# Finer waits at four seams of a two-block kernel, and filter generation moved ahead of the inverse transform's matmul

## The chip, the cores and the metric

The kernel runs on one core of a Trainium2 chip, as one launch. The metric is the device time of an execution in microseconds (us). Three runs of the kernel before took 3126.72, 3129.09 and 3131.32 us; their median is 3129.09 us.

The engines in the text: PE (TensorE matmul, with PEld its weight loads), DVE (VectorE), ACT (ScalarE), POOL (GpSimd) and SP (SyncE). POOL and SP issue the DMAs. Each engine runs its own instructions in the order in which they are written, and waits on counting semaphores.

## The reference

Input x is 2048 rows by 1024 channels, float32. A first block (banded attention and a pooled path) is followed by a second, in which the whole change lies. Cut to what matters:

```python
h = rms_norm(x, pre_norm_w)
proj = h @ w_in                       # 1024 -> 7168
hy_in, hy_gate, sg_u, sg_v, sg_gate = split(proj)
hy_in = short_conv_centred(hy_in, conv_w, conv_b)   # u[t-1]*w0 + u[t]*w1 + u[t+1]*w2 + b
x0, x1, v = split(hy_in, 3)
k = hyena_filter(...)                 # 3-layer sine MLP -> (4096, 1024) samples, * decay, / l1 norm
y_a = x0 * long_conv_bidir(v * x1, k, hyena_skip) * silu(hy_gate)   # FFT convolution over 4096
# spatial gating: per head (8 heads of 128), LayerNorm of sg_v, then a 128 x 128 mix along time
mixed = einsum('hpq,bnqhd->bnphd', sgu_w, vc) + sgu_b
y_b = sg_u * mixed * silu(sg_gate)
x = x + rms_norm(concat(y_a, y_b) @ w_out, post_norm_w)
```

## The kernel before

The second block has three parts, which follow one another in program order; between blocks of the program all engines meet.

**Projections (some 970 to 2242 us).** After the values (sg_v) the projections run as a list of tiles, each 128 output channels by 2048 rows in four PSUM banks, two tiles in flight (banks 0 to 3 and 4 to 7). A projection tile takes 8 x 4 x 3 matmuls (lines L1845 to L1847, high and low halves of the operands). The first 24 tiles are, for each head h, `gate`, `mix`, `u`; the rest are, for each channel group e, `x0`, `hgate`, `x1`, `v` (with one tile `third` of the filter network). Before PE writes tile j it waits for the evacuation of tile j-2 (`banks_free`).

- A `mix` tile is 16 matmuls (L1822) over VN, the normalised values of one head. POOL loads VN in one DMA of 1024 KB (L1666), double buffered; VN lies over the output buffer of the head before, so that the load for head h first waits until the result of head h-1 is stored. PE waits for the whole load.
- A convolution tile (`x0`, `x1`, `v`) is evacuated by ACT with the middle tap (L1715), then DVE adds the two outer taps (L1740, L1743). For `v` DVE then forms the product (L1784) that SP stores.
- DVE puts 6 to 14 operations of the filter network's first layer (`filter_work`, L120 to L143) behind each tile, and splits the weights of the tile after next (L1730).

**Long convolution (2242 to 2770 us), `long_convolution`.** Channels go in four chunks of 256 (NCH = 4). The 32 filter samples of a chunk are generated in 16 steps: PE `generate` (L2332) into one PSUM bank, DVE `weighted` times the decay (L2176), ACT absolute value (L2086), DVE `summed` (L2185). For the first chunk this is done up front. For the later ones one step lies in each of the 16 pairs of the chunk before. `generate(n + 16)` waits until `weighted(n + 15)` has read the bank.

Pair n of a chunk is: PE `forms` (L2406: filter spectrum, then input spectrum), ACT four copies of the filter spectrum (L2124, L2126), DVE three products and a difference (L2263, L2264, L2265, L2267), then `weighted` and `summed`; PE `inverse` (L2390), ACT `inverse_out` (L2106). PE runs ahead by one: in step p it issues forms(p+1), inverse(p-1), generate(p+16). ACT's order is the copies of pair p, inverse_out(p-1), absolute value, copies of pair p+1.

Between two chunks PE transforms the next filter (`filter_first`, L2344, 16 groups, four banks ahead of DVE's transposes L2193 in `filter_turned`), transposes the next inputs (`inputs_turn`, L2367), runs `inverse_first` (L2432) and `inputs_first` (L2377). DVE also turns the outputs (`outputs_turned`, L2210), the inputs (`inputs_turned`, L2202), and applies `gate` (L2227) and `gate_product` (L2239).

**Output projection (2742 to 3128 us)**, L2532 to L2534, which the change doesn't touch.

Of the kernel before, what the change touches and what calls it, by code (L numbers as in the profile page):

```python
# [9 lines left out]
ALU = mybir.AluOpType  # L10
# [5 lines left out]
S = 2048  # L16
# [1155 lines left out]
def second_inputs(nc, A, PS, first, first_ctx, CC, HP, kept, h1_d, h2_d, vn_d, bi_d, u_d, gx_d, yb_d, wv_d):  # L1172

    with ExitStack() as outer:
# [404 lines left out]
        with ExitStack() as ctx:  # L1579
# [10 lines left out]
            sgt_in = [stage_sem("sgt_in%d" % i) for i in range(2)]  # L1590
            vn_in = stage_sem("vn_in")
            mix_gated = stage_sem("mix_gated")
# [9 lines left out]
            arg3_done = stage_sem("arg3_done")  # L1602
            sin3_done = stage_sem("sin3_done")
            CONV = ("x0", "x1", "v")
            CONV_AT = {"x0": 0, "x1": 1, "v": 0}
# [45 lines left out]
            @block.gpsimd  # L1651
            def _(g):
                values_gpsimd(g)
                for b in range(2):
                    g.wait_ge(vn_stored[b], 16 * NT)
                g.wait_ge(sv_done, STEPS)
                g.sem_clear(first.semaphores)
                vnr = vn_d.rearrange("(i p) (h d) -> h p i d", p=P, d=P)
                for h in range(8):
                    if h >= 2:  # L1660
                        g.wait_ge(sgu_done, h - 1)
                    g.dma_start(SGT[:, h % 2], A["sgu_w_2"][h]).then_inc(sgt_in[h % 2], 16)
                    g.dma_start(BI[:, h % 2], bi_d[h]).then_inc(sgt_in[h % 2], 16)
                    if h:
                        g.wait_ge(yb_stored[(h + 1) % 2], 16 * ((h + 1) // 2))
                    g.dma_start(VN[h % 2], vnr[h]).then_inc(vn_in, 16)  # L1666

            @block.scalar
            def _(s):
# [10 lines left out]
                for j, (kind, n, _) in enumerate(tiles):  # L1680
# [7 lines left out]
                    if kind not in ("u", "mix"):  # L1688
                        s.wait_ge(tile_done, j + 1)
# [7 lines left out]
                    elif kind == "hgate":  # L1697
                        if n:
                            s.wait_ge(u_stored, 16 * n)
                        else:  # L1700
                            s.wait_ge(yb_stored[1], 64)
                        s.activation(AB[1], ps, ACT.Silu).then_inc(evac_done, 1)
                    elif kind in CONV:
                        which = CONV.index(kind)
# [17 lines left out]
            def _(v):  # L1722
# [10 lines left out]
                def outer_taps(which, n, j):  # L1733
# [11 lines left out]
                    v.wait_ge(taps_done, conv + 1)  # L1745

                def second_angle():
# [18 lines left out]
                for j, (kind, n, _) in enumerate(tiles):  # L1766
# [5 lines left out]
                    elif kind == "mix":  # L1772
# [6 lines left out]
                        v.wait_ge(evac_done, evacs_before(j))  # L1779
                        v.tensor_tensor(AB[n % 2], ps, AB[n % 2], ALU.mult).then_inc(mix_gated, 1)  # L1780
                    elif kind in CONV:
                        outer_taps(CONV.index(kind), n, j)
# [17 lines left out]
            def _(t):  # L1800
# [13 lines left out]
                for j, (kind, n, _) in enumerate(tiles):  # L1814
# [3 lines left out]
                    if kind == "mix":  # L1818
                        t.wait_ge(sgt_in[n % 2], 32 * (n // 2 + 1))
                        t.wait_ge(vn_in, 16 * (n + 1))  # L1820
                        for i in range(NT):
                            ins = t.matmul(PS[:, banks + i // 4, P * (i % 4):P * (i % 4) + P], VN[n % 2][:, i], SGT[:, n % 2],  # L1822
                                           start=True, stop=True)
# [7 lines left out]
                    else:  # L1831
                        w = slot_of[j]
                        t.wait_ge(wl_done, NV + w + 1)
                        for c in range(NTC):
# [7 lines left out]
                            for k in range(KD):  # L1842
# [4 lines left out]
                                ins = t.matmul(dst, wl, hh, start=False, stop=(k == KD - 1))  # L1847
                    ins.then_inc(tile_done, 1)

# [22 lines left out]
def long_convolution(nc, A, CC, HP, KX, M, PS, kept, L, gx_d, u_d, ya_d, yb_d):  # L1872

    with ExitStack() as ctx:
# [287 lines left out]
        def _(v):  # L2162
# [41 lines left out]

            def outputs_turned(ug):
                cc, ct = ug // 2, ug % 2
                v.wait_ge(z_done, 16 * cc + 16)
                for h in range(2):
                    c = P * ct + 64 * h
                    v.transpose(KTC[cc % 2][:, c:c + 64], UTC[:, c:c + 64]).then_inc(it_done, 1)  # L2210
# [44 lines left out]
            for cc in range(NCH):  # L2255
# [33 lines left out]
                if cc + 1 < NCH:  # L2289
# [3 lines left out]
                    summed(16 * cc + 31)  # L2293
                    filter_turned(cc + 1, range(2, 8))
                outputs_turned(2 * cc)
                if cc + 1 < NCH:
                    filter_turned(cc + 1, range(8, 16))
                    norm(cc + 1)
# [11 lines left out]
        def _(t):  # L2310
# [45 lines left out]
            def inputs_turn(ug):  # L2356
                t.wait_ge(uin_in, 16 * (ug + 1))
                if ug % 2 == 0:
                    t.wait_ge(kt_done, 8 * ug + 16)
                else:  # L2360
                    t.wait_ge(ut_done, 4 * ug)
                for q in range(4):
# [31 lines left out]
            def second_stage(cc):  # L2394
# [469 lines left out]
```

## Time and profile before

| | us |
|---|---|
| median of three runs | 3129.09 |
| the profiled execution, its own time | 3130.32 |
| its span | 3128.5 |
| PE busy | 2982.3 (95%) |
| DVE busy | 2531.5 (81%) |
| ACT busy | 827.0 (26%) |
| granted PE clock, mean share of full speed | 0.987 |

The span is the time between the first and the last recorded instruction; 1.8 us of the execution lie around it. A PE idle time is given with the engine, DMA or tile that ended it.
### The profile page before, as it was taken

The numbers are of one execution on the slowest core, as the hardware profiler recorded it, in microseconds if no ns is written. First come the engines' busy times: TensorE is split into PE (matmuls) and PEld (weight loads), VectorE is DVE, ScalarE is ACT, GpSimd is POOL, SyncE is SP. The second block draws the span as 40 slices with busy tenths as digits, with TensorE's granted clock in tenths as the row PEclk, the third lists the DMA queues.
The fourth block names the chain that finished last, engine by engine and source line by source line (L and its number), as shares of the span: only waits on it lengthen the run. The fifth ranks groups of instructions, "written<-read, shape, count | busy, mean of one in ns | idle before, by whom it ended". The sixth has DMA issues, their size and how long they took to land. (4 is left out here: it accounts for less than half of the span.)

```text
span 3128.5 us, 33046 instructions
## 1 busy us (share of the span) xinstructions
PE 2982.3 (95%) x12866; PEld 2163.7 (69%) x12866; DVE 2531.5 (81%) x2789; ACT 827.0 (26%) x1402; POOL 336.1 (11%) x458
## 2 busy tenths in 40 slices
PE   8999999999998999999999999999899989889999
PEld 4444444656777887888888888887656656678887
DVE  7979999898996869999999999998477979762221
ACT  3000000696334320000011111112343735631111
POOL 2211121001333430000000000000000100000000
PEclk9999999999999999999999999999999999989999
DMA  7675553201457546565554454541222331454331
GB/s 214 180 172 158 174 151 79 115 1 65 148 186 241 145 134 171 150 182 141 153 140 139 122 152 135 141 141 34 109 86 81 110 120 42 148 168 124 92 108 41
DMA packets 212115, 406.39 MB, mean 130 GB/s; under 512 B 21008, under 2 KB 134328, under 8 KB 204088
## 3 DMA queue, kind: packets, MB, share of 16 engines
q1 hardware_dynamic: 189256, 324.58, 34.2%
q0 software_dynamic: 21552, 71.32, 8.4%
q10 hardware_dynamic: 1152, 8.39, 0.7%
q8 instruction: 102, 1.67, 0.2%
q14 instruction: 53, 0.43, 0.0%
HBM read 324.53 MB, written 85.98 MB: 131 GB/s over the span
## 5 line engine op out<-in xcount | busy, mean ns | idle before, releaser
L1845 PE MATMUL PS<-HX,WH 128*128 128x512 f32 x1536 | 599.4, 390 | 6.9 <-DVE MB L1743 5.0
L1847 PE MATMUL PS<-HX,WL 128*128 128x512 f32 x1536 | 598.3, 390 | 0.0
L1846 PE MATMUL PS<-HX,WH 128*128 128x512 f32 x1536 | 598.3, 390 | 0.0
L849 PE MATMUL PS<-M 128*128 128x512 f32 x1088 | 472.0, 596 | 7.5 <-DVE M L650 6.3
L849 PEld LDWEIGHTS PS<-M 128*128 128x128 f32 x1088 | 207.4, 191 | 271.9 <-issue 263.7
L1845 PEld LDWEIGHTS PS<-HX,WH 128*128 128x128 f32 x1536 | 288.9, 188 | 67.9 <-DVE MB L1743 5.9
L1846 PEld LDWEIGHTS PS<-HX,WH 128*128 128x128 f32 x1536 | 288.9, 188 | 59.9
L1847 PEld LDWEIGHTS PS<-HX,WL 128*128 128x128 f32 x1536 | 288.7, 188 | 60.0
L120 DVE SCALAR_TENSOR_TENSOR HP<-MF,HP 128x1024 f32<-128x1024 f32 x252 | 323.5, 1284 | 8.0
L120 DVE SCALAR_TENSOR_TENSOR M<-M 128x1024 f32<-128x1024 f32 x160 | 205.6, 1285 | 26.5 <-DMA M<-c_feat 20.9
L2532 PE MATMUL PS<-WH,YH 128*128 128x512 f32 x512 | 202.1, 395 | 8.9 <-DVE HP L2671 5.2
L2533 PE MATMUL PS<-WH,YL 128*128 128x512 f32 x512 | 201.4, 393 | 0.0
L2534 PE MATMUL PS<-WL,YH 128*128 128x512 f32 x512 | 201.2, 393 | 0.0
L2655 DVE TENSOR_TENSOR YL<-KX,YH 128x2048 fp32r<-128x2048 f32 x14 | 32.1, 2292 | 205.2 <-ACT YH L2634 205.2
L1715 ACT ACTIVATE MB<-PS,MF 128x2048 f32<-128x2048 f32 x24 | 49.6, 2066 | 444.5 <-PE PS L1847 444.5
L2062 POOL DMA_DIRECT2D M<-c_decay x48 | 25.8, 538 | 1095.7 <-DVE KX L2176 893.9
L72 POOL DMA_DIRECT2D M<-c_feat x186 | 94.9, 515 | 382.5 <-DVE M L120 361.8
L2532 PEld LDWEIGHTS PS<-WH,YH 128*128 128x128 f32 x512 | 97.4, 190 | 31.6 <-issue 7.4
L1530 PE MATMUL PS<-WVH,HX 128*128 128x512 f32 x256 | 101.4, 396 | 14.2 <-DVE HX L1454 6.0
L1028 DVE TENSOR_TENSOR M<-M 128x1024 f32<-128x1024 f32 x90 | 110.1, 1223 | 2.4
L2534 PEld LDWEIGHTS PS<-WL,YH 128*128 128x128 f32 x512 | 97.4, 190 | 20.4
L2533 PEld LDWEIGHTS PS<-WH,YL 128*128 128x128 f32 x512 | 97.4, 190 | 20.3
(224 smaller groups left out, 5060.7 us busy)
## 6 DMA issues: line engine op xcount, KB each, us to landing
MF<-h_scratch SPq DMA_DIRECT2D x380, 256.0 KB, 4.3
M<-c_feat POOLq DMA_DIRECT2D x186, 256.0 KB, 4.4
MF<-w_in SPq DMA_DIRECT2D x52, 512.0 KB, 4.8
M<-u_scratch SPq DMA_DIRECT2D x16, 1024.0 KB, 4.9
M<-c_decay POOLq DMA_DIRECT2D x48, 256.0 KB, 2.9
M<-x SPq DMA_DIRECT2D x18, 512.0 KB, 4.1
M<-w_in SPq DMA_DIRECT2D x18, 512.0 KB, 5.9
x_scratch<-M SPq DMA_DIRECT2D x16, 512.0 KB, 5.0
```

The costliest lines, as they stand in the source:

```text
L72: eng.dma_start(dst[HID * half:HID * half + HID], row).then_inc(loaded, 16)
L120: return v.scalar_tensor_tensor(out=out, in0=a, scalar=s_, in1=b, op0=op0, op1=op1)
L849: ins = t.matmul(ps[:, c, :], wt[:, k], HT[:, k, TC * c:TC * c + TC], start=(k == 0), stop=(k == KD - 1))
L1028: link(v.tensor_tensor(out, a, b, op))
L1530: t.matmul(dst, hh, wh, start=(k == 0), stop=False)
L1715: s.activation(AB[CONV_AT[kind]], ps, ACT.Identity, bias=w[:, 3:4], scale=w[:, 1:2]).then_inc(evac_done, 1)
L1845: t.matmul(dst, wh, hh, start=(k == 0), stop=False)
L1846: t.matmul(dst, wh, hl, start=False, stop=False)
L1847: ins = t.matmul(dst, wl, hh, start=False, stop=(k == KD - 1))
L2532: t.matmul(dst, yh, wh, start=(n == 0), stop=False)
L2533: t.matmul(dst, yl, wh, start=False, stop=False)
L2534: return t.matmul(dst, yh, wl, start=False, stop=(n == KY - 1))
```

## The change

Five edits, all in the second block:

1. VN is loaded by two DMAs of 8 time blocks each, with a semaphore each; PE waits for the second ahead of the ninth matmul of a `mix`.
2. The last projection tile (`v`, 7) is evacuated in two halves of 1024 columns: ACT, two taps and product for the first half once PE has finished its two banks, then for the second.
3. In `outputs_turned` for the chunk's first 128 channels the two transposes are put apart: after filter groups 0 to 5 and 0 to 10, where both stood behind group 7.
4. `inputs_turn` for the odd channel group waits for three of the four transposes of the even one; `inputs_first` waits for the fourth ahead of its second group.
5. In the pairs of the first three chunks `generate` stands in front of `inverse`.

```diff
@@ gpsimd, loads of the mix
-                    g.dma_start(VN[h % 2], vnr[h]).then_inc(vn_in, 16)
+                    for half in range(2):
+                        g.dma_start(VN[h % 2][:, 8 * half:8 * half + 8], vnr[h][:, 8 * half:8 * half + 8]).then_inc(vn_in[half], 16)
@@ scalar
+                    elif (kind, n) == LAST_TILE:
...
+                        for half in range(2):
+                            s.wait_ge(last_half_done, half + 1)
+                            part = slice(1024 * half, 1024 * half + 1024)
+                            s.activation(AB[0][:, part], ps[:, part], ACT.Identity, bias=w[:, 3:4], scale=w[:, 1:2]).then_inc(last_evac, 1)
@@ vector
+                def last_tile(ps, w):
+                    dst = AB[0]
+                    for half, (lo, hi) in enumerate(((0, 1023), (1023, S))):
+                        first, end = 1024 * half, 1024 * half + 1024
+                        v.wait_ge(last_evac, half + 1)
+                        v.scalar_tensor_tensor(out=dst[:, max(first, 1):end], in0=ps[:, max(first, 1) - 1:end - 1], scalar=w[:, 0:1],
+                                               in1=dst[:, max(first, 1):end], op0=ALU.mult, op1=ALU.add).then_inc(last_tap, 1)
...
+                        ins = v.tensor_tensor(AB[1][:, lo:hi], dst[:, lo:hi], AB[1][:, lo:hi], ALU.mult)
+                    ins.then_inc(u_done, 1)
@@ tensor, a mix tile
-                        t.wait_ge(vn_in, 16 * (n + 1))
                         for i in range(NT):
+                            if i % 8 == 0:
+                                t.wait_ge(vn_in[i // 8], 16 * (n + 1))
@@ vector, between two chunks
-                    filter_turned(cc + 1, range(2, 8))
-                outputs_turned(2 * cc)
-                if cc + 1 < NCH:
-                    filter_turned(cc + 1, range(8, 16))
+                    filter_turned(cc + 1, range(2, 6))
+                    outputs_turned(2 * cc, (0,))
+                    filter_turned(cc + 1, range(6, 11))
+                    outputs_turned(2 * cc, (1,))
+                    filter_turned(cc + 1, range(11, 16))
                     norm(cc + 1)
@@ inputs_turn
-                    t.wait_ge(ut_done, 4 * ug)
+                    t.wait_ge(ut_done, 4 * ug - 1)
@@ inputs_first
+                    elif g == 1 and ug % 2:
+                        t.wait_ge(ut_done, 4 * ug)
@@ second_stage, the loop over pairs
+                    if cc + 1 < NCH:
+                        generate(n + 16)
                     if p >= lag_of(cc):
                         inverse(n - lag_of(cc))
-                    if cc + 1 < NCH:
-                        generate(n + 16)
```

On PE, in a pair of the first chunk, the rows before are these (L2406 is forms, L2390 inverse, L2332 generate):

```order
L2390 MATMUL PS<-M3 128x256 x2
L2332 MATMUL PS<-M3,HP 64x256 x4
L2406 MATMUL PS<-KX,M3 128x256 x2
L2406 MATMUL PS<-M3 128x256 x2
L2390 MATMUL PS<-M3 128x256 x2
```

And these in the changed kernel, where L2442 is forms, L2366 generate and L2426 inverse:

```order
L2442 MATMUL PS<-KX,M3 128x256 x2
L2442 MATMUL PS<-M3 128x256 x2
L2366 MATMUL PS<-M3,HP 64x256 x4
L2426 MATMUL PS<-M3 128x256 x2
L2442 MATMUL PS<-KX,M3 128x256 x2
```

The four matmuls of generate now stand between forms and the inverse of the pair before.

On DVE, between the first and the second chunk, the rows before are these (L2193 turns filter groups, L2185 adds up absolute values, L2210 turns outputs, L2215 and L2217 are the norm):

```order
L2193 STREAM_TRANSPOSE M<-PS 128x16x16x2
L2185 TENSOR_TENSOR M<-M 128x512
L2193 STREAM_TRANSPOSE M<-PS 128x16x16x2 x6
L2210 STREAM_TRANSPOSE KX<-M 128x64x16x2 x2
L2193 STREAM_TRANSPOSE M<-PS 128x16x16x2 x8
L2215 TENSOR_SCALAR M<-PS 128x1 x2
L2217 RECIPROCAL M<-M 128x2
```

And these in the changed kernel (L2226 filter groups, L2243 outputs, L2248 and L2250 the norm):

```order
L2226 STREAM_TRANSPOSE M<-PS 128x16x16x2
L2218 TENSOR_TENSOR M<-M 128x512
L2226 STREAM_TRANSPOSE M<-PS 128x16x16x2 x4
L2243 STREAM_TRANSPOSE KX<-M 128x64x16x2
L2226 STREAM_TRANSPOSE M<-PS 128x16x16x2 x5
L2243 STREAM_TRANSPOSE KX<-M 128x64x16x2
L2226 STREAM_TRANSPOSE M<-PS 128x16x16x2 x5
L2248 TENSOR_SCALAR M<-PS 128x1 x2
```

The two long transposes, which stood together behind filter group 7, now have five filter groups between them.

## Rows read from the trace of the kernel before

**Rows 1.** Who waited for whom, PE: us in total, times, longest us.

```profile
PE PS L1822 <- DMA MB<-vn_scratch: 10.7, 4, 3.1
PE PS L2332 <- PEq L1579: 10.1, 1, 10.1
PE PS L2367 <- DVE M L2202: 5.7, 4, 1.4
```

**Rows 2.** PE in a pair, timeline: start us, us, engine, line, operation.

```profile
2326.41 1.13 PE L2332 MATMUL PS<-M,HP 64*64 64x256 f32 x8
2327.47 1.18 PE L2406 MATMUL PS<-KX,M 128*128 128x256 f32 x4
...
2329.40 1.07 PE L2390 MATMUL PS<-M 128*128 128x256 f32 x4
2330.39 1.13 PE L2332 MATMUL PS<-M,HP 64*64 64x256 f32 x8
```

**Rows 3.** DVE in the same pair, timeline.

```profile
2328.23 0.69 DVE L2267 TENSOR_TENSOR M<-M 128x512 f32<-128x512 f32 x1
2328.84 0.68 DVE L2176 TENSOR_TENSOR M<-PS,M 128x512 f32<-128x512 f32 x1
...
2330.08 0.69 DVE L2263 TENSOR_TENSOR M<-PS,M 128x512 f32<-128x512 f32 x1
```

**Rows 4.** ACT in the same pair, timeline; in brackets idle before, and releaser.

```profile
2327.56 1.19 ACT L2124 ACTIVATE M<-PS 64x512 f32<-64x512 f32 x2
2328.78 1.21 ACT L2126 ACTIVATE M<-PS 64x512 f32<-64x512 f32 x2
2330.50 0.65 ACT L2106 ACTIVATE M<-PS 128x512 f32<-128x512 f32 x1 [0.51 <-PE PS L2390]
```

**Rows 5.** PE windows, first chunk's generation: stretch, length, busy, clock, DMA share, GB/s.

```profile
2250.00:2266.00 16.00, 12.12 (x88) 1.00 0.76 308
```

**Rows 6.** PE and DVE timeline between two chunks; DVE's waits, 2377 to 2393.

```profile
2386.62 5.41 PE L2344 MATMUL PS<-M 128*128 128x512 f32 x8 [2.33 <-DVE M L2193]
2381.50 4.46 DVE L2210 STREAM_TRANSPOSE KX<-M 128x2048 f32<-128x2048 f32 x2
DVE M L2193 <- PE PS L2344: 1.7, 3, 1.0
```

**Rows 7.** Windows of PE at two places behind a wait.

```profile
2388.00:2390.00 2.00, 2.00 (x4) 0.50 0.00 0
...
1303.00:1305.00 2.00, 2.00 (x11) 0.50 1.03 240
```

**Rows 8.** Input transposes between two chunks, PE and DVE, timeline.

```profile
2411.57 1.14 PE L2367 MATMUL PS<-M 128*128 128x128 f32 x8 [1.44 <-DVE M L2202]
2408.43 1.25 DVE L2202 STREAM_TRANSPOSE M<-PS 128x1024 f32<-128x1024 f32 x1 [0.49 <-PE PS L2377]
```

**Rows 9.** Last projection tile: ACT and DVE, timeline; a 1024-wide operation by form.

```profile
2232.64 2.06 ACT L1715 ACTIVATE MB<-PS,MF 128x2048 f32<-128x2048 f32 x1 [19.69 <-PE PS L1847]
2239.57 2.29 DVE L1784 TENSOR_TENSOR MB<-MB 128x2048 f32<-128x2048 f32 x1
L2671 DVE SCALAR_TENSOR_TENSOR HP<-PS,SSQ,KX 128x1024 f32<-128x1024 f32 x16 | 20.5, 1284 | 44.8 <-POOL SSQ L2627 44.8
```

**Rows 10.** ACT behind the tiles of heads 2 and 3, timeline; POOL's load.

```profile
1252.63 1.88 ACT L1694 ACTIVATE MB<-PS 128x2048 f32<-128x2048 f32 x1 [20.70 <-PE PS L1847]
...
1277.97 1.06 ACT L1672 ACTIVATE WH<-MF 128x1024 fp32r<-128x1024 f32 x1 [22.52 <-PE PS L1847]
1299.73 1.88 ACT L1694 ACTIVATE MB<-PS 128x2048 f32<-128x2048 f32 x1 [20.70 <-PE PS L1847]
...
1329.15 1.06 ACT L1672 ACTIVATE WH<-MF 128x1024 fp32r<-128x1024 f32 x1 [26.60 <-PE PS L1847]
1291.70 1.17 POOL L1666 DMA_DIRECT2D MB<-vn_scratch  x1 [47.34 <-DMA yb_scratch<-MB]
```

**Rows 11.** DVE's waits from 1204 to 1504 us.

```profile
DVE WL L1730 <- ACT WH L1672: 7.9, 3, 3.0
```

More of the change, by code:

```diff
@@ L1590, in second_inputs @@
             sgt_in = [stage_sem("sgt_in%d" % i) for i in range(2)]
-            vn_in = stage_sem("vn_in")
+            vn_in = [stage_sem("vn_in%d" % i) for i in range(2)]
             mix_gated = stage_sem("mix_gated")
@@ L1603, in second_inputs @@
             sin3_done = stage_sem("sin3_done")
+            last_half_done = stage_sem("last_half_done")
+            last_evac = stage_sem("last_evac")
+            last_tap = stage_sem("last_tap")
+            LAST_TILE = ("v", 7)
             CONV = ("x0", "x1", "v")
@@ L1687, in _ @@
                         s.activation(L3[2][HID:P, 1:S], L3[1][HID:P, S - 1:0:-1], ACT.Sin).then_inc(sin3_done, 1)
-                    if kind not in ("u", "mix"):
+                    if kind not in ("u", "mix") and (kind, n) != LAST_TILE:
                         s.wait_ge(tile_done, j + 1)
@@ L1702, in _ @@
                         s.activation(AB[1], ps, ACT.Silu).then_inc(evac_done, 1)
+                    elif (kind, n) == LAST_TILE:
+                        w = CW[:, 8 * CONV.index(kind) + n]
+                        s.wait_ge(gx_stored, 16 * (n + 1))
+                        for half in range(2):
+                            s.wait_ge(last_half_done, half + 1)
+                            part = slice(1024 * half, 1024 * half + 1024)
+                            s.activation(AB[0][:, part], ps[:, part], ACT.Identity, bias=w[:, 3:4], scale=w[:, 1:2]).then_inc(last_evac, 1)
                     elif kind in CONV:
@@ L1745, in outer_taps @@
                     v.wait_ge(taps_done, conv + 1)
+                def last_tile(ps, w):
[5 more added lines that the diff above has]
+                                               in1=dst[:, max(first, 1):end], op0=ALU.mult, op1=ALU.add).then_inc(last_tap, 1)
+                        v.wait_ge(last_tap, 2 * half + 1)
+                        stop = min(hi, S - 1)
+                        v.scalar_tensor_tensor(out=dst[:, lo:stop], in0=ps[:, lo + 1:stop + 1], scalar=w[:, 2:3],
+                                               in1=dst[:, lo:stop], op0=ALU.mult, op1=ALU.add).then_inc(last_tap, 1)
+                        v.wait_ge(last_tap, 2 * half + 2)
+                        ins = v.tensor_tensor(AB[1][:, lo:hi], dst[:, lo:hi], AB[1][:, lo:hi], ALU.mult)
+                    ins.then_inc(u_done, 1)
                 def second_angle():
@@ L1780, in _ @@
                         v.tensor_tensor(AB[n % 2], ps, AB[n % 2], ALU.mult).then_inc(mix_gated, 1)
+                    elif (kind, n) == LAST_TILE:
+                        last_tile(ps, CW[:, 8 * CONV.index(kind) + n])
                     elif kind in CONV:
@@ L1847, in _ @@
                                 ins = t.matmul(dst, wl, hh, start=False, stop=(k == KD - 1))
-                    ins.then_inc(tile_done, 1)
+                            if (kind, n) == LAST_TILE and c % 2:
+                                ins.then_inc(last_half_done, 1)
+                    if (kind, n) != LAST_TILE:
+                        ins.then_inc(tile_done, 1)
             first_ctx.close()
@@ L2203, in inputs_turned, with outputs_turned @@
                                 PS[:, 2 * (g % 2):2 * (g % 2) + 2, :].rearrange("p x (c i) -> p c x i", i=16)).then_inc(ut_done, 1)
-            def outputs_turned(ug):
+            def outputs_turned(ug, halves=(0, 1)):
                 cc, ct = ug // 2, ug % 2
                 v.wait_ge(z_done, 16 * cc + 16)
-                for h in range(2):
+                for h in halves:
                     c = P * ct + 64 * h
```

## The prediction

> **What bounds the kernel now.** I read the engines' busy shares first: PE has work in 95% of the span, so only what PE waits for, or how slowly it is clocked, can be won. Then the list of PE's waits [rows 1]: 10.7 us for the loads of the mix tiles, one wait of 10.1 us at the seam between projections and convolution, 5.7 us in four waits for turned inputs. Then the timeline of each of these places, and last, since edit 5 moves work in 45 pairs, the timeline of one pair on three engines [rows 2 to 4]. There the reader is to see that a pair takes 3.98 us: generate starts at 2326.41 and again at 2330.39 [rows 2], and no idle time stands before PE's or DVE's rows [rows 2, 3]. ACT waits 0.51 us for inverse in each pair [rows 4].
>
> **Edit 5, generate ahead of inverse.** Generate takes 1.06 us (2326.41 to the next start, 2327.47), inverse 0.99 (2329.40 to 2330.39) [rows 2]. PE's own sum doesn't change. What changes is a circle of waits over two pairs. Follow it: inverse starts; ACT's inverse_out starts 1.10 later (2329.40 to 2330.50) [rows 2, 4]; inverse_out and the absolute value take 1.04 (the period of 3.98 less the four copies, 2327.56 to 2328.78 + 1.21 = 2.43, less the idle 0.51) [rows 4]; the four copies 2.43; DVE's products start 0.09 behind them (2329.99 to 2330.08) [rows 3, 4]; DVE ends weighted 3.42 after it began its pair (2330.08 less 3.98 is 2326.10; 2328.84 + 0.68 is 2329.52) [rows 3]. So from inverse(p-1), in PE's step p, to weighted of pair p+1 there are 1.10 + 1.04 + 2.43 + 0.09 + 3.42 = 8.08 us. PE's step p+2 then issues generate, which must wait for that weighted (one bank), some 0.06 more, and inverse(p+1).
>
> Before, inverse comes first and needs only the difference, which DVE finishes 0.60 ahead of weighted (2328.23 + 0.69 is 2328.92) [rows 3]; the circle is then 8.08 - 0.60 + 0.06 = 7.54 for two pairs, under the 7.96 that PE's own work takes, so it doesn't bind. After, generate stands in the circle: 8.08 + 0.06 + 1.06 = 9.20 for two pairs, 4.60 per pair, over 3.98. Neither ACT nor DVE can shorten it, because each executes in order: the copies of pair p+1 are queued behind inverse_out(p-1) on ACT, and DVE's next pair behind the copies. The circle starts with the chunk's first generate that waits. The pairs 0 and 1 start as before; pair 2 starts when its copies, queued behind inverse_out(0), are done: weighted(0) at DVE's start + 3.42, 0.06 + 1.06 for generate, then 1.10 + 1.04 + 2.43 + 0.09, together 9.20 behind the start of pair 0; by the same sum it was 7.54. From pair 3 to pair 15 lie six more circles. That makes 1.66 at the start and 6 x (9.20 - 7.96) = 7.44: 9.1 us per chunk, for three chunks +27.3. A generate that has waited may be slower by 0.1, as its weights aren't loaded ahead: 0.7 per chunk. From below the bound is 0 (the circle doesn't close), from above 31. I take +27.5. Nothing hides it: the transform of the next filter waits for the last weighted of the chunk, and the last chunk, without generate, isn't touched.
>
> **Edit 3, halves of the turned outputs.** PE waits 2.33 us for a turned filter group behind DVE's two long transposes (4.46), and its eight instructions then take 5.41 us [rows 6]; for four of these microseconds it is at 1.2 GHz in part, [rows 7] show 0.50. PE could win 2.33 and some 1.9 of clock, 4.2 in all. But DVE has all 16 groups and the same 4.46 to do, and what follows waits for its last group. It is idle 1.7 us in this stretch [rows 6], and by my estimate some 0.6 more between the first eight groups, where it follows PE in steps under the list's threshold. So DVE bounds the gain at 2.3. In the new order it comes to that: half a transpose (2.2) lies under three matmul groups of PE. -2.3 three times, -7; bounds -5 and -12.
>
> **Edit 4.** PE waits 1.44 us for the fourth input transpose [rows 8], in all 5.7 at four places [rows 1]. The third has ended at 2408.43 + 1.25 = 2409.68, before PE's preceding matmuls are issued (about 2410.0), so the wait goes wholly, with some 0.1 of restart: -1.5 four times, -6. The fourth is late next only for inputs_first, 25 us on. Bounds: 0 and -6.4.
>
> **Edit 2, the last tile.** From PE's end the path is ACT 2.06 (from 2232.64), two taps, the product (to 2239.57 + 2.29 = 2241.86): 9.2 us [rows 9]. The first half now runs under PE's second (half of a tile's 21 us, the idle time of ACT before such a tile's end in [rows 10]). The second half costs: ACT 1.05, taps 1.28 each by the 1024-wide form, product 1.22 (half of 2.29 and a little) and 0.2 of releases: 5.0 [rows 9]. -4.2. DVE is idle there, so nothing is queued behind. Bounds -3.5 and -4.6. The clock falls in the remaining wait as before.
>
> **Edit 1, halves of the mix loads.** Behind an even head gate and u end 25.34 us apart (1252.63 to 1277.97), behind an odd one 29.42 (1299.73 to 1329.15) [rows 10]. Of the 4.08 the wait for the load is some 2.2 by the timeline (on average 10.7 / 4 = 2.7 [rows 1]); the rest is clock: 0.50 from 1303 on [rows 7]. If each of the four odd heads loses that, it is 16.3 in all, of which 10.7 are waits [rows 1]. The load takes 10.2 us (from 1291.70 to the end of PE's wait, 1299.7 + 2.2) [rows 10]; its first half should be there some 4 us earlier, an estimate from half of that, and eight matmuls of 0.23 then cover 1.9 of what is left. But DVE has little room: it waited 7.9 us in three waits, one per two heads [rows 11], so that two heads can shrink by 2.6 at most, and the load itself starts behind DVE's product. So: 2.6 three times at the most for heads up to 6, and 3 to 4 for head 7, behind which the convolution tiles leave DVE room: 11. If the clock still falls behind the second half's wait, 1.9 each is kept, partly under DVE: 7. I take -9.5, between; bounds 0 and -14. SP and its queue aren't touched; POOL issues two DMAs for one, and nothing is queued behind them that is due.
>
> **The sum.** +27.5 - 7 - 6 - 4.2 - 9.5 = +0.8 us on the profiled execution's 3130.3: 3131.1. That execution lies 1.2 over the median of the runs shown, so 3129.9 in terms of the median. A measurement of this kernel can tell about 0.2%, 6.3 us, from no change.
>
> **Rivals.** (a) The pairs keep their 3.98 us: the circle is not closed, since a wait that I read as binding is met early. Then edit 5 costs nothing, perhaps wins the 1.4 us waits at the chunks' ends, and the time is 3129.9 - 27.5 = 3102. For it speaks that ACT has 0.51 us idle per pair and PE waits for inverse at the ends of the chunks; against it that DVE starts 0.09 behind ACT's copies already, without room.
>
> (b) Slower: DVE paces the gate, mix and u tiles. The place is heads 0 to 7, the price is that edit 1 gives back at most 1 instead of 9.5: 3129.9 + 9 = 3139. For it: a DVE waiting only 7.9 us in 300 [rows 11], and a second half that lands no earlier than the whole did. Against: the clock cost, which is PE's own. It is slower than before beyond the 6.3 from the point where edit 1 gives less than 4.
>
> (c) The clock falls in the pairs. They would have idle of about 1.2 us in 9.2. In the first chunk's generation PE is busy 12.12 of 16 us in short pieces and keeps 1.00 [rows 5]; one fall costs about 1.9, as at the mixes, and a fall per circle, 21 times, would add 40 and give 3170. The Trainium skill speaks for this one: its page "TensorE: Matmul & The Clock Gate", section "A second HAM failure mode: psum-queue depth-cycling", says that short idles between groups of matmuls, from cycling through PSUM banks, can make the clock oscillate. The trace agrees that waits can bring the clock down [rows 7], but not in a stretch that is busier on average than the one of [rows 5].
>
> **Numbers.** Forecast 0.67, with an own range of 3121 to 3139; (a) 0.14; (b) 0.14; (c) 0.05. Within the forecast the sizes of edits 1 and 5 are each uncertain by 4 or so, together 6: of its 0.67 some 0.49 lies within 6.3 us, 0.10 under and 0.08 over. Rival (a) adds 0.14 to faster, (b) 0.05 to same and 0.09 to slower, (c) 0.05 to slower. Faster 0.24, same 0.54, slower 0.22. The range 3115 to 3141 leaves out most of (a) and (c).
>
> **What would show it.** In the changed profile: DVE's first product of every second pair 9.2 us apart instead of 7.96; PE idle before generate, released by weighted, of about 1.2 every second pair, and none before inverse at the chunks' ends but the last. No wait of 2.3 us in the filter's transform, and the clock at 1.00 there. Four waits for input transposes gone. The seam's wait 5.9 us instead of 10.1. At the odd mixes no wait before the first matmul, one of some 1 to 2.5 before the ninth. Pairs at 3.98 us would make the forecast wrong by the whole of edit 5, and odd heads that still take 29 us by edit 1.

## The result, and the profile after

The changed kernel takes 3147.64 us (median of 4 runs, 3144.01 to 3151.18) against 3128.42 of the kernel before on the same chip: ratio 1.0056, 95% interval 1.0043 to 1.0068. It is 19.2 us slower, 17.7 over the forecast of 3129.9 and outside the range, and it is slower where no change was forecast. The profiled execution took 3146.14 us.

The engines' busy times on the page of the changed kernel, and its clock in the view of the cores:

```profile
PE 2995.2 (95%) x12866; PEld 2171.8 (69%) x12866; DVE 2531.6 (81%) x2792; ACT 826.2 (26%) x1403; POOL 341.1 (11%) x466
...
core 0: 3144.3 us, clock 0.984
```

DVE has the same work as before. PE has 12.9 us more (2982.3 before), though the change adds no matmul to it, and its clock went from 0.987 to 0.984. Busy time that grows without work is the first sign of a lower clock.

PE's waits in the changed kernel (us in total, times, longest us), where L2366 is generate, L1852 the mix and L2442 forms:

```profile
PE PS L2366 <- DVE M L2209: 22.6, 16, 3.1
PE PS L2366 <- DVE KX L2209: 14.5, 19, 2.7
PE PS L2366 <- PEq L1579: 6.0, 1, 6.0
PE PS L2442 <- DVE M L2235: 5.7, 4, 1.4
...
PE PS L1852 <- DMA MB<-vn_scratch: 4.2, 6, 1.2
...
PE PS L2401 <- ACT M L2127: 2.3, 8, 0.3
```

Against [rows 1]: the mixes wait 4.2 us instead of 10.7 and at most 1.2 at a time, the seam waits 6.0 instead of 10.1, and the 5.7 us of inputs_turn (L2401) for DVE are gone. The row of the same size for forms (L2442) was there before and isn't touched by the change. Generate's wait for weighted (L2209) is 37 us in two rows, against 3.2 before, which is what the circle of edit 5 says. In return the inverse waits 3.7 us for DVE's difference instead of 14.8:

```profile
PE PS L2390 <- DVE M L2267: 14.8, 9, 2.1
```

```profile
PE PS L2426 <- DVE M L2300: 3.7, 3, 1.4
```

The first of these rows is of the kernel before (L2390), the second of the changed kernel.

The circle itself, PE of the changed kernel in the first chunk (start us, us, engine, line, operation, in brackets idle before and its releaser):

```profile
2323.56 1.13 PE L2366 MATMUL PS<-M,HP 64*64 64x256 f32 x8 [1.28 <-DVE M L2209]
2324.62 1.17 PE L2426 MATMUL PS<-M 128*128 128x256 f32 x4
...
2327.53 1.14 PE L2366 MATMUL PS<-M,HP 64*64 64x256 f32 x8
...
2332.85 1.14 PE L2366 MATMUL PS<-M,HP 64*64 64x256 f32 x8 [1.28 <-DVE M L2209]
```

DVE and ACT in the same pairs:

```profile
2324.05 0.69 DVE L2296 TENSOR_TENSOR M<-PS,M 128x512 f32<-128x512 f32 x1
...
2329.38 0.69 DVE L2296 TENSOR_TENSOR M<-PS,M 128x512 f32<-128x512 f32 x1 [1.30 <-issue]
...
2333.35 0.69 DVE L2296 TENSOR_TENSOR M<-PS,M 128x512 f32<-128x512 f32 x1
```

```profile
2325.83 0.63 ACT L2139 ACTIVATE M<-PS 128x512 f32<-128x512 f32 x1 [1.87 <-PE PS L2426]
...
2329.81 0.62 ACT L2139 ACTIVATE M<-PS 128x512 f32<-128x512 f32 x1 [0.52 <-PE PS L2426]
```

Two pairs take 9.29 us (2323.56 to 2332.85), where the forecast had 9.20 and the kernel before 7.96 [rows 2]. Every second generate waits 1.28, the one between doesn't: PE waits for weighted, then ACT for the inverse (1.87), then DVE, by the order of the program, for ACT's copies (1.30; the profile names no releaser there). All three engines have idle time in it, so none of them is the bound; the circle is.

What the forecast didn't have stands between the chunks. PE of the changed kernel behind chunk 0: L2378 is filter_first, L2387 the sums of the norm, L2401 inputs_turn, L2468 inverse_first, L2413 inputs_first.

```profile
2366.14 15.01 PE L2378 MATMUL PS<-M 128*128 128x512 f32 x30
2381.73 1.14 PE L2378 MATMUL PS<-M 128*128 128x512 f32 x2 [0.58 <-DVE M L2226]
...
2384.22 1.14 PE L2401 MATMUL PS<-M 128*128 128x128 f32 x8 [0.52 <-DVE M L2226]
2385.64 1.66 PE L2401 MATMUL PS<-M 128*128 128x128 f32 x8 [0.28 <-ACT M L2127]
2387.09 13.75 PE L2468 MATMUL PS<-M,KX 128*128 128x64 f32 x64
2400.63 8.48 PE L2413 MATMUL PS<-M 128*128 128x512 f32 x16
...
2411.37 7.65 PE L2468 MATMUL PS<-M,KX 128*128 128x64 f32 x64
```

PE windows over the fall and behind it (stretch, length, busy of PE, PEld, DVE, ACT, POOL, then the clock, DMA share, GB/s):

```profile
2386.00:2404.00 18.00, 18.00 (x77) 16.10 (x76) 7.61 (x7) 1.42 (x3) 0.00 (x0) 0.53 0.16 58
2404.00:2415.00 11.00, 10.73 (x60) 7.63 (x58) 7.15 (x6) 2.35 (x4) 0.00 (x0) 1.00 0.21 67
```

Edit 3 did what it says: the wait of 2.33 us [rows 6] became 0.58 + 0.52. But the 64 narrow matmuls behind it take 13.75 us at 1.2 GHz, and 7.65 us at 2.4 GHz one stage later. The clock stays low for 17 us in a stretch in which PE never waits; behind the one long wait of the kernel before it was low for 3.4 (counted in windows of 1 us; [rows 7] show it at 2388).

Over the chunks, the windows from 2306 to 2742 us, the changed kernel and then the kernel before:

```profile
2306.00:2742.00 436.00, 385.19 (x1731) 264.19 (x1730) 336.94 (x445) 212.98 (x361) 22.04 (x41) 0.94 0.27 94
```

```profile
2306.00:2742.00 436.00, 394.20 (x1849) 269.79 (x1850) 364.45 (x483) 240.71 (x406) 23.65 (x44) 0.98 0.27 95
```

A mean clock of 0.94 over 436 us is 52 us at 0.50, against 17 before. Half of such time is lost where PE works; where PE waits, the low level costs nothing.

### The profile page after: what moved, and what is told of

The parts are those of the page before. It is cut to its first block and busy times, and to the rows that moved or that the text cites. A ratio compares the mean times of both kernels' runs of the same rounds, so it can differ in the third digit from the quotient of the medians.

```text
span 3144.3 us, 33058 instructions
## 1 busy us (share of the span) xinstructions
PE 2995.2 (95%) x12866; PEld 2171.8 (69%) x12866; DVE 2531.6 (81%) x2792; ACT 826.2 (26%) x1403; POOL 341.1 (11%) x466
## 5 line engine op out<-in xcount | busy, mean ns | idle before, releaser
L120 DVE SCALAR_TENSOR_TENSOR M<-M 128x1024 f32<-128x1024 f32 x160 | 205.6, 1285 | 27.5 <-DMA M<-c_feat 22.0
```

The source lines that it names most:

```text
L120: return v.scalar_tensor_tensor(out=out, in0=a, scalar=s_, in1=b, op0=op0, op1=op1)
```

## The experiments

Two figures for each kernel below: its median, and its "0.50 time", the median over its runs of twice (1 - mean clock) times the time. Half the 0.50 time is taken as what the low level costs, and the median of time less that half is called "at full clock". The clock is given to 0.001, which is 6 us of 0.50 time, so that a figure at full clock is good to some 3 us. It is an estimate, and in one way off: low level that lies under a wait of PE costs nothing and is counted all the same. Added up from windows of 0.25 us in each kernel's one trace, that is 13 to 27 us (22 in the kernel before). "Before" is the kernel before on the same chip. Its medians there are 3128.4 to 3130.2 us in five sets of runs; in the four whose clocks are on record it has 75 to 81 us of 0.50 time and 3089 to 3091 at full clock. Kernels of different sets are best compared by their ratios. Line numbers are each kernel's own.

| kernel | median us (runs) | ratio to before, 95% | 0.50 time | at full clock |
|---|---|---|---|---|
| changed kernel, edits 1 to 5 | 3147.64 (4) | 1.0043 to 1.0068 | 101 | 3097.9 |
| gen_behind, edits 1 to 4 | 3116.27 (9) | 0.9938 to 0.9972 | 94 | 3071.4 |
| gen_only, edit 5 | 3160.29 (4) | 1.0091 to 1.0120 | 89 | 3115.3 |
| filled_idle | 3135.78 (6) | 1.0014 to 1.0036 | 66 | 3103.0 |
| gen_ahead_middle | 3128.44 (10) | 0.9992 to 1.0016 | 66 | 3092.4 |
| mix_halves_only, edit 1 | 3121.55 (7) | 0.9963 to 0.9984 | 75 | 3084.6 |
| last_halves_only, edit 2 | 3123.71 (8) | 0.9972 to 0.9996 | 69 | 3089.6 |
| outputs_halves_only, edit 3 | 3138.45 (12) | 0.9996 to 1.0038 | 107 | 3085.7 |
| inputs_wait_only, edit 4 | 3122.82 (12) | 0.9966 to 0.9987 | 81 | 3083.1 |
| after_without_3, edits 1, 2, 4, 5 | 3143.84 (5) | 1.0029 to 1.0058 | 82 | 3101.7 |
| edits_1_2_4 | 3114.73 (5) | 0.9936 to 0.9964 | 75 | 3074.6 |
| seams_filled | 3112.62 (5) | 0.9934 to 0.9961 | 75 | 3077.3 |
| edits_1_2_4_filled | 3108.89 (5) | 0.9924 to 0.9949 | 56 | 3080.9 |
| outputs_halves_filled | 3131.60 (12) | 0.9996 to 1.0020 | 85 | 3089.1 |
| edits_1_to_4_filled | 3106.50 (5) | 0.9911 to 0.9936 | 62 | 3075.4 |

**Edit 5 taken back, and edit 5 alone.** gen_behind is the changed kernel with the old order in the pairs; gen_only is the kernel before with the new one.

```diff
@@ gen_behind against the changed kernel
-                    if cc + 1 < NCH:
-                        generate(n + 16)
                     if p >= lag_of(cc):
                         inverse(n - lag_of(cc))
+                    if cc + 1 < NCH:
+                        generate(n + 16)
```

> The changed kernel with edit 5 undone alone: generate stands behind inverse again. Theory (the circle of waits lengthens the pairs, and the idle it brings lets the clock fall around the chunks' ends and starts): pairs at 3.98 us again, clock at 0.50 for about as long as in the kernel before between 2242 and 2742 us; the segments of the two traces give -10.8 (mix tiles), -3.9 (seam), -2 (first chunk) and -11 to -17 (three seams between chunks) against the kernel before: 3100 us, 3094 to 3105. Rival (edits 3 and 4 bring the clock falls, by moving the transposes): the falls stay, and the time is about 3120.

> The kernel before with edit 5 alone: generate ahead of inverse. Theory: the circle costs 27 us and the clock about 20 more, 3170 to 3180 us against 3128. Rival (the falls need edits 3 or 4 as well): 3128 + 27 = 3155.

Edit 5 costs 30.4 us alone and 31.4 on top of the others; at full clock 25 and 26.5. With the low level under PE's waits left out of the count (22 us before, 27 in gen_only; 16 in gen_behind, 21 in the changed kernel), it is some 28 and 29. gen_only, at 3160, lies between its theory (3170 to 3180) and its rival (3155). In gen_behind the pairs are back at 3.98 us without idle time, PE's timeline there:

```profile
2322.22 1.13 PE L2366 MATMUL PS<-M,HP 64*64 64x256 f32 x8
...
2326.20 1.13 PE L2366 MATMUL PS<-M,HP 64*64 64x256 f32 x8
```

But gen_behind is at 3116, not at the 3100 expected, and nearer to the rival's 3120, by which edits 3 and 4 bring the falls: edits 1 to 4 give 13.6 us, where the forecast had 26.7. Its trace, with no edit 5 in it, has the long fall behind chunk 2:

```profile
2627.84 13.76 PE L2468 MATMUL PS<-M,KX 128*128 128x64 f32 x64
```

**Idle time filled, and edit 5 in part.** filled_idle is the changed kernel with matmuls whose results nobody uses, in the circles and at both ends of the chunks: the forms of the input spectrum twice in every even pair, those of the filter spectrum too in pair 2, and four matmuls behind pair 15. gen_ahead_middle has generate ahead of the inverse in pairs 3 to 12 only.

```diff
@@ filled_idle, in forms
-                        for x in range(2):
-                            ins = t.matmul(PS[:, bank, CH * x:CH * x + CH], STRIP[:, 2 * p + x], src[:, p, x], start=True, stop=True)
+                        again = cc + 1 < NCH and p % 2 == 0 and p and (p == 2 or formed is uf_done)
+                        for _ in range(1 + again):
+                            for x in range(2):
+                                ins = t.matmul(PS[:, bank, CH * x:CH * x + CH], STRIP[:, 2 * p + x], src[:, p, x], start=True, stop=True)
@@ gen_ahead_middle, the loop over pairs
-                    if cc + 1 < NCH:
+                    if cc + 1 < NCH and 3 <= p <= 12:
                         generate(n + 16)
                     if p >= lag_of(cc):
                         inverse(n - lag_of(cc))
+                    if cc + 1 < NCH and not 3 <= p <= 12:
+                        generate(n + 16)
```

> The changed kernel with matmuls added where PE idles: the input-spectrum matmuls of every second pair are issued twice (0.9 us), both spectra of pair 2 twice, and at a chunk's last pair four matmuls go into two banks that nobody reads. The values are the same. PE has 3 x 9.9, some 30 us more to do. Theory (the clock falls because PE idles): the circle is unchanged since it waits for DVE anyway, the falls at the chunks' starts and ends go, and the kernel becomes faster than the changed one by 10 to 20 us: 3128 to 3138. Rival (the clock falls for another reason, or its level doesn't matter to a PE that waits): as slow as the changed kernel, 3148, or slower by what the added matmuls lengthen.

> The changed kernel, but generate ahead of inverse only in pairs 3 to 12 of a chunk, behind it in pairs 0 to 2 and 13 to 15. Theory (circle): five circles of 9.2 instead of 7.96 per chunk, 6 us per chunk, so 18 over the kernel with generate behind; the long idles at the chunks' starts and ends go, and with them most falls of the clock: about 3118. Rival (the idle of 1.3 us in every second pair is what lets the clock fall at the end): falls at the chunks' ends stay, and about 3130.

With more matmuls to execute, filled_idle is 11.9 us faster than the changed kernel: 5 us slower at full clock, and 35 us less of 0.50 time. That the clock costs something here, and that PE's waits in and around the pairs bring on part of its falls, is shown by this run: the waits in the seams are not filled in it. gen_ahead_middle is within 0.2% of the kernel before: 3128, where its theory said 3118 and its rival 3130. Its 0.50 time did go down, from 101 us to 66, as the theory had it. At full clock it is 21 us over gen_behind, where 18 were expected; the 3118 was built on gen_behind at 3100, which came at 3116.

**Each edit alone.**

> The kernel before with edit 1 alone (the mix loads in halves). Theory: it gives what the trace of the changed kernel shows up to the wait of the last head's tiles, about -11 us against the kernel before, because the waits of 10.7 us shrink and the falls of the granted clock behind odd heads (0.50 in a 1-us window, about 10 us of such windows in all before) go away; in the profile the first wait at the odd mixes is gone. The stretch of 0.50 windows in the convolution stage stays as it was, as nothing there is touched: ratio about 0.9965. Rival (b) of the prediction: DVE paces the heads and the edit gives at most 1 us. Second rival: the gain of 11 is partly lost because the clock falls elsewhere in the convolution, then the profile shows more windows at 0.50 behind 2300 than the 30 or so of before.

> The kernel before with edit 2 alone (the last projection tile in halves). Theory: -4 us (4.2 forecast, and the changed kernel's seam was 3.9 us shorter beyond what the mixes gave), the wait at the seam 6 us instead of 10; the clock at 0.50 behind it for less than the 10 us of before. That would be a ratio of 0.9987, within what can be told from none. Rival: the shorter wait lets the clock fall later, in the first generation of filters, and the edit gives nothing.

> The kernel before with edit 3 alone (the turned outputs in halves among the groups of the filter's turn). Theory: the wait of 2.3 us before the filter's transform goes in three chunks, but the time gained is under the 7 us forecast, 3 to 5 us, because the many short waits of PE at DVE's transposes now stand where one long wait stood, and the granted clock falls there or behind (0.50 windows at 2386 to 2404 in the changed kernel, 17 us, against 3.4 in the kernel before). Rival: the full 7 us and no added windows at 0.50, the 17 us of them then belong to edit 5 or to chance.

> The kernel before with edit 4 alone (inputs_turn waits for three of the four transposes). Theory: the four waits of 1.4 us go, the fourth transpose is waited for one group later, where PE has at most 0.4 us of other work in front, so that about 0.8 us of each 1.4 come back there; -2 to -3 us in all. Rival: the forecast of -6 us, all four waits gone and nothing in their place. At either size the ratio lies between 0.998 and 1, so the profile's waits decide: waits of PE at inputs_turn, and those before the second inputs group.

Edit 1 gives 8.6 us, edit 2 6.5, edit 4 7.4, each with an interval of some 3 to 4 either way. Edit 3 costs 8.3; its interval reaches from -1 to +12, so that the median alone does not show a cost, but neither its theory (3 to 5 gained) nor its rival (7 gained) holds. For edit 4 the forecast's -6 was nearer than the -2 to -3 expected here: in its seam nothing waits for DVE any more.

```profile
2401.35 1.05 PE L2367 MATMUL PS<-M 128*128 128x128 f32 x8
2402.68 1.25 PE L2367 MATMUL PS<-M 128*128 128x128 f32 x8 [0.28 <-ACT M L2094]
2403.77 7.65 PE L2434 MATMUL PS<-M,KX 128*128 128x64 f32 x64
```

Edit 3 alone repeats the long fall of the changed kernel, in two places, behind chunks 1 and 2. PE behind chunk 2, where L2345 is filter_first and L2433 inverse_first:

```profile
2635.16 14.82 PE L2345 MATMUL PS<-M 128*128 128x512 f32 x30
2650.56 1.13 PE L2345 MATMUL PS<-M 128*128 128x512 f32 x2 [0.59 <-DVE M L2193]
...
2653.05 1.14 PE L2368 MATMUL PS<-M 128*128 128x128 f32 x8 [0.52 <-DVE M L2193]
2654.46 1.79 PE L2368 MATMUL PS<-M 128*128 128x128 f32 x8 [0.28 <-ACT M L2094]
2656.06 13.75 PE L2433 MATMUL PS<-M,KX 128*128 128x64 f32 x64
```

PE windows over both falls (length, busy, clock, DMA share, GB/s):

```profile
2538.00:2556.00 18.00, 17.83 (x76) 0.53 0.47 176
2654.00:2672.00 18.00, 17.72 (x77) 0.53 0.17 58
```

The fall behind chunk 1 lies elsewhere, on the second of the seam's two narrow stages, behind a wait that the kernel before has too. The first stage there, behind waits of 0.51 and 0.28, takes 8.49:

```profile
2519.78 8.49 PE L2433 MATMUL PS<-M 128*128 128x64 f32 x64
...
2536.74 1.14 PE L2368 MATMUL PS<-M 128*128 128x128 f32 x8 [1.44 <-DVE M L2202]
...
2539.62 13.76 PE L2433 MATMUL PS<-M 128*128 128x64 f32 x64
```

Behind chunk 0 the same three short waits as behind chunk 2 stand in the same order in this run, and the stage takes 7.65. So the same waits were followed by no fall, by a short one and by a long one: they don't bring the long fall each time. That its runs scatter so much fits this. Its twelve, in order of 0.50 time:

| 0.50 time | 69 | 75 | 75 | 75 | 100 | 107 | 107 | 113 | 113 | 113 | 126 | 145 |
|---|---|---|---|---|---|---|---|---|---|---|---|---|
| us | 3123.2 | 3120.2 | 3125.2 | 3125.8 | 3131.6 | 3137.4 | 3141.9 | 3139.5 | 3142.2 | 3144.8 | 3146.9 | 3158.5 |

From 75 to 145 us of 0.50 time the runs grow by 33 to 38 us, half of the difference. The four with as little as the kernel before are 4 to 10 us under its median: there edit 3 seems to give its gain, as far as four runs can tell.

The traces of all kernels together bear on what edit 3 has to do with the long fall. Each has six narrow stages in its three seams between chunks. A stage of 13.75 us or so stands in 3 of the 5 traces of kernels that have edit 3 with its waits unfilled (four stages: one in the changed kernel, one in gen_behind, two here), in none of the 8 without edit 3, and in none of the 3 with its waits filled.

**Edit 3 taken out.** after_without_3 is the changed kernel with the old order of the output transposes, edits_1_2_4 is gen_behind with it.

> The changed kernel with edit 3 taken back (edits 1, 2, 4 and 5). Theory now: edit 3 costs about 8 us, as alone (3138.5 against 3130.2), because the falls of the granted clock it causes lie on the first stage of the inverse (64 matmuls of 64 columns: 13.75 us instead of 7.65, 17.1 us at 0.50 instead of 3.4). Then this kernel takes 3147.6 - 8 = 3139 to 3140, a ratio of 1.003, and its six instances of that stage all take 7.65. Rival: edit 3 cost something only in its own run, and here it gives back the 4 to 7 us of waits as forecast: then this kernel takes 3151 to 3154.

> The kernel before with edits 1, 2 and 4. Theory: the single edits add up, -8.6, -6.5 and -7.4, so 3130 - 22.5 = 3107.5 us, a ratio of 0.993, and it beats the 3116.3 of edits 1 to 4; the first stage of the inverse takes 7.65 everywhere. Rival: the gains overlap in the clock (each edit alone took some falls away that the others take too) and it stays at 3112 to 3117, as edits 1 to 4 did.

Taking edit 3 out of the changed kernel gives 3.8 us (101 us of 0.50 time to 82), half of what its cost alone had led me to expect, and the intervals of the two ratios overlap; out of gen_behind it gives 1.5, which can't be told from nothing. The single gains don't add up either: 8.6 + 6.5 + 7.4 = 22.5, and the three together give 13.9. At full clock they do within the error (5.4 + 0.4 + 6.9 = 12.7, together 14.7; by my estimate some 17 and 17 with the low level under waits left out); what doesn't add up is the clock. Alone, edits 1 and 2 took 6 and 13 us off the 0.50 time; together with edit 4 nothing is taken off (75 and 75). The rival in the expectation of edits_1_2_4, that the gains overlap in the clock, has its time (3112 to 3117) and fits these figures.

**Fills at the seams and at the pairs' ends.** A fill in the seam is a matmul of 256 columns into a free bank, five of them behind each of chunks 0, 1 and 2; at the pairs' ends the four forms of pair 2 are issued twice, and four matmuls lie around the last generate.

```diff
@@ filter_first, seams_filled and outputs_halves_filled
+                    if cc and g == 15:
+                        seam_filler(2)
@@ inputs_turn
+                if fill:
+                    seam_filler(2)
...
+                    if fill and q == 2:
+                        seam_filler(1)
```

> Edits 1 to 4 (generate behind the inverse), and matmuls whose results nobody uses, put in front of the short waits of the seam behind chunks 0 and 1: two of 128x256 before the last group of the filter's transform, two before inputs_turn, one in its middle, 1.4 us in each of three chunks, all on waits of 0.59, 0.52 and 0.28 us. Theory (the short waits bring on the fall that then lies on the inverse's first stage): that stage takes 7.65 everywhere, the windows at 0.50 fall by a third, and the time goes from 3116.3 to about 3108. Rival: the falls come from DVE's pace or from chance and don't ask for these waits; then 3116 to 3119 and an instance of 13.75 is still there.

> Edits 1, 2 and 4, and matmuls whose results nobody uses at both ends of each chunk's pairs: the four forms of pair 2 twice, and at pair 15 two before the inverse and two behind the last generate, 2.2 us of them a chunk, put on waits of 1.3 to 2.8 us. Theory: falls at the chunks' ends go (in the same filling of the changed kernel the 0.50 windows went from 100 to 66 us and the time from 3147.6 to 3135.8), so 5 to 9 us under the kernel with edits 1, 2 and 4: 3100. Rival: the fillers cost PE time that isn't idle, and it is no faster than edits 1, 2 and 4.

> The kernel before with edit 3 alone, and in the three seams behind chunks 0, 1 and 2 matmuls whose results nobody uses: two of 128x256 before the last group of the filter's transform, two before inputs_turn, one in its middle. Theory (the short waits of 0.59, 0.52 and 0.28 us, which edit 3 puts ahead of the inverse's first stage, bring on the fall of the clock that then lies on it): the 0.50 windows go from the 107 us of edit 3 alone to about 80, and the time from 3138.5 to 3125 to 3128, under the kernel before. Rival: the falls come from something else in edit 3 (the order of DVE's work, or chance in the run), the fills cost up to 1.4 us a chunk, and it stays at 3137 to 3142.

> Edits 1 to 4 (generate behind the inverse) with the fills of both places, the seams' and the pairs' ends. Theory: both add up, 3112.6 (seams filled) less the 5.8 that the fills at the pairs' ends gave edits 1, 2 and 4 (3114.7 to 3108.9): 3106 to 3107; as edit 3 is worth about 3 us once the clock is out of it, it then beats edits 1, 2 and 4 filled, 3108.9. Rival: at the remaining falls (34 us of windows at 0.50 in that kernel's trace from 1100 on) there is nothing more to fill, and with edit 3 the time is 3109 to 3112.

edits_1_2_4_filled is the clearest case: 5.8 us faster than edits_1_2_4 in the same set, within the 5 to 9 expected though not at 3100, with no overlap between their runs (3108.2 to 3109.9 against 3111.3 to 3115.2) and 56 us of 0.50 time instead of 75. outputs_halves_filled has a median 6.9 us under edit 3 alone: 3.4 slower at full clock, 22 us less of 0.50 time. It lies between theory (3125 to 3128) and rival (3137 to 3142), and the intervals of the two ratios overlap. In its trace no stage of 13.75 is left, but three of its twelve runs still have 101 to 113 us of 0.50 time. That the seam's short waits bring on a part of the falls fits this and the traces above, but no time shows it by itself; where the others come from stays open. seams_filled is 3.7 under gen_behind (8 expected), less than its margin, and no stage of 13.75 is left in its trace either.

The seam behind chunk 0 in edits_1_to_4_filled, where L2372 are the fills:

```profile
2360.85 13.54 PE L2384 MATMUL PS<-M 128*128 128x512 f32 x30
2374.23 1.02 PE L2372 MATMUL PS<-M 128*128 128x256 f32 x4
2375.09 1.03 PE L2384 MATMUL PS<-M 128*128 128x512 f32 x2
...
2376.81 1.11 PE L2372 MATMUL PS<-M 128*128 128x256 f32 x4
2377.76 1.06 PE L2412 MATMUL PS<-M 128*128 128x128 f32 x8
2378.66 0.60 PE L2372 MATMUL PS<-M 128*128 128x256 f32 x2
2379.11 1.26 PE L2412 MATMUL PS<-M 128*128 128x128 f32 x8
```

No idle time is left ahead of the narrow stage. This kernel, edits 1 to 4 with both fills, is the fastest tried: 3106.50 us, 22.8 under the kernel before and 41 under the changed one, and within the 3106 to 3107 expected. It is 2.4 faster than edits_1_2_4_filled, which was timed in another set and has no fills in the seams. That edit 3 is worth having once its waits are filled is likely by this, but not shown: edits 1, 2 and 4 with both fills weren't run.

## Why the prediction was wrong

| edit | forecast | alone | of it at full clock |
|---|---|---|---|
| 5 | +27.5 | +30.4 | +25.2 |
| 3 | -7 | +8.3 | -4.3 |
| 4 | -6 | -7.4 | -6.9 |
| 2 | -4.2 | -6.5 | -0.4 |
| 1 | -9.5 | -8.6 | -5.4 |
| sum | +0.8 | +16.2 | +8.2 |

The column at full clock counts all 0.50 time as costly, also what lies under PE's waits.

**Edit 5** was right: the circle, its engines and its length (9.29 us against 9.20), also in gen_only, and with it rival (a) falls. Its size was 3 to 4 us short. By the figures that leave out the low level under waits, most of that is clock: 0.50 time around the chunks' ends, which the term didn't have. The 0.1 us allowed for a generate that has waited isn't there: it takes 1.06 us to the next start behind a wait and 1.07 without one.

**Edit 3** is the step that failed. It said that "PE could win 2.33 and some 1.9 of clock", and that the gain would be -7. The waits shrank as worked out. The clock went the other way: alone the edit adds 26 us of 0.50 time, 13 us of time. The step took the fall behind a wait as belonging to that wait and its length, so that a shorter wait could only help. In the kernel before the one wait of 2.33 us was followed by 3.4 us of low clock, on wide matmuls. In the changed kernel waits of 0.58, 0.52 and 0.28 were followed by 17, on 64 narrow ones, whose stage took 6.1 us longer. This came in some seams and some runs only, and what sets the length of a fall isn't shown: neither the waits nor the narrow matmuls by themselves do, since the same waits ahead of the same stage were also followed by none. With the other edits beside it edit 3 didn't give its 7 us but cost 1.5 to 3.8, each of them hardly told from nothing. Measured so, its term is 8.5 to 10.8 of the 17.7 us of the miss, the largest part but not the whole.

**Edits 1 and 2** were sized about right alone. Edit 2's wait is 6.0 us in the trace instead of 10.1, which is the 4.2 forecast; its median moved by 6.5, with an interval from 1.3 to 8.8. The -0.4 at full clock does not say that its gain is clock. In the kernel before 5.1 us of the low level at this seam lie inside the wait, and 1.3 with edit 2; behind the wait it lasts 5.1 and 5.5. In the whole trace 22 us lie under waits before and 13 with edit 2, so that by this estimate some 5 us of its gain are waits. For edit 1 the heads behind an odd head's gate are 13.0 us shorter in the changed kernel's trace, those behind an even head's 2.2 longer (gate to u on ACT, four each), -10.8 in all. Part of the 2.2 is a wait that the forecast didn't have, at the mix of an even head, in PE's timeline of the changed kernel:

```profile
1250.20 2.05 PE L1852 MATMUL PS<-MB 128*128 128x128 f32 x16 [0.55 <-DMA MB<-vn_scratch]
```

DVE paces it only in part, so rival (b), at most 1 us, is wrong. In company edits 1, 2 and 4 give 13.9 instead of the 19.7 forecast for them: the 1.9 us of clock per mix that edit 1 counted doesn't stay won, and falls turn up elsewhere (75 us of 0.50 time, as before). **Edit 4** was right, and a little more.

**Rival (c)** had the right sign and mechanism and the wrong place. The clock did fall in the convolution (0.94 against 0.98 over 436 us), and falls stand at the chunks' ends. The Trainium skill's page "TensorE: Matmul & The Clock Gate", section "A second HAM failure mode: psum-queue depth-cycling", has short idles between groups of matmuls make the clock oscillate; the trace agrees at the chunks' ends. But the circles with their waits of 1.28 us every 9.29 keep 1.00 in most places. The falls lie at the ends and beginnings of the chunks, where waits of 1.3 to 3 us come close together, and at the seams. It had a chance of 0.05. One such place is the start of chunk 1 in the changed kernel, PE's timeline and its window:

```profile
2437.88 1.98 PE L2366 MATMUL PS<-CC,HP 64*64 64x256 f32 x8 [2.72 <-DVE KX L2209]
2439.79 2.07 PE L2426 MATMUL PS<-M 128*128 128x256 f32 x4
```

```profile
2437.00:2445.00 8.00, 7.12 (x22) 4.67 (x24) 4.09 (x7) 3.03 (x6) 1.08 (x2) 0.57 0.80 287
```

Generate takes 1.98 us there and the inverse 2.07 (the chunk's pairs have 1.13 and 1.17).

Another division of the same 17.7 us, as an estimate: some 7 are terms that were too good even at full clock (+8 instead of +0.8, mainly in edits 1 and 3), and the other 11 are 0.50 time added to the kernel (101 us instead of 75, which makes 13 by that figure, where none was counted). Why falls come in some runs and not in others of the same kernel isn't settled.

## What to carry to other kernels

A wait that is cut into several shorter ones isn't a smaller cost until the clock behind them has been looked at: read the windows behind the wait, and above all whether long runs of narrow matmuls follow, which take 1.8 times as long at the low level. Compare two versions at their 0.50 time as well as at their median; when it differs beyond the scatter of the runs, the edit may have moved falls about, and then single gains need not add up. Before giving PE a new operation between a result and the engine that waits for it, add up the circle over all engines: here it gave 9.20 us for two pairs and the trace had 9.29. A low clock costs only where the engine works: look whether a fall lies under a wait before counting it.

## What the hardware showed beyond expectation

- Useless matmuls in PE's idle time made the changed kernel 11.9 us faster, edits 1, 2 and 4 5.8 (3114.73 to 3108.89) and edits 1 to 4 9.8 (3116.27 to 3106.50).
- Three waits of 0.59, 0.52 and 0.28 us ahead of a stage can be followed by 17 us at 1.2 GHz with PE busy throughout; the stage of 64 matmuls with 64 columns took 13.75 us instead of 7.65. The same waits were also followed by no fall at all.
- The same kernel (gen_behind) took 3103.3 to 3123.9 us, in step with its mean clock: its four runs at 0.989 or more took 3103.3 to 3109.7, the others, at 0.983 to 0.985, 3116 to 3124.
